# Openings of five stages: two weight splits on GpSimd, the mean in another place, one more split ahead

## The reference, cut to what matters

```python
h = h + 0.5 * rmsnorm_2(swiglu(rmsnorm_2(h, g[0]), w_ffn_in, w_ffn_out), g[1])
hn = rmsnorm_2(h, g[2])
mix = gla_mixer(hn, ...)            # or swa_mixer
h = h + rmsnorm_2(mix, g[3])
# rmsnorm_2: x * rsqrt(mean(x * x) + EPS) * g
```

## Time and profile before

| | us |
|---|---|
| median of 3 runs | 1802.15 (1801.6 to 1804.75) |
| profiled execution, its own time | 1803.02 |
| its span in the trace | 1801.2 |
| PE busy | 1742.8 (97%) |
| DVE busy | 1236.5 (69%) |
| ACT busy | 915.5 (51%) |
| POOL busy | 138.5 (8%) |
| mean granted clock of PE | 0.986 |

### The profile page before, as it was taken

One profiled execution on the slowest core, in us unless ns is written; L12 is line 12 of the kernel. 1 busy time (PEld: TensorE's weight loads), 2 busy tenths in 40 slices (PEclk: granted clock), 3 DMA queues, 4 the chain that ended last, 5 costly groups with the idle time before them and its releaser, 6 DMA issues.

```text
span 1801.2 us, 32903 instructions
## 1 busy us (share of the span) xinstructions
PE 1742.8 (97%) x13432; PEld 1646.8 (91%) x13432; DVE 1236.5 (69%) x2050; ACT 915.5 (51%) x1612; POOL 138.5 (8%) x179
## 2 busy tenths in 40 slices
PE   7999999998899999999999999999999998999998
PEld 6999999888589998999989889999899996699998
DVE  7977786765877666766466468665676657777664
ACT  7656455433764455544445445444554545555442
POOL 2001320200010001000010021000200011020001
PEclk9999999998999999999999999999999998999999
DMA  5215656541035556555544234555455562145553
GB/s 174 83 35 188 233 179 199 187 137 63 1 119 187 187 189 206 170 174 175 191 137 152 73 116 162 173 172 193 144 176 185 190 200 93 48 152 188 187 192 125
DMA packets 76469, 276.34 MB, mean 153 GB/s; under 512 B 8672, under 2 KB 9824, under 8 KB 76192
## 3 DMA queue, kind: packets, MB, share of 16 engines
q1 hardware_dynamic: 75168, 270.57, 45.4%
q0 software_dynamic: 288, 2.30, 0.4%
q10 hardware_dynamic: 864, 1.38, 0.2%
HBM read 273.16 MB, written 1.05 MB: 152 GB/s over the span
## 4 chain that ended last, share of the span: by engine, by line
PE 82%; DVE 13%; ACT 2%; issue 2%; DMA 2%; ACTq 0%; DVEq 0%
PE acc L1921 43%; PE mix L1921 18%; PE acc L1917 5%; PE acc L1918 3%; DVE scr L413 3%; DVE wl L2202 2%; DVE xl L2214 2%; DMA arrived<-in_w 1%; DVE x L2240 1%; PE acc L1941 1%; DVE y L2234 1%; PE mix L2007 1%; PE mix L807 1%; PE acc L1963 1%; ACT wh L2060 1%
## 5 line engine op out<-in xcount | busy, mean ns | idle before, releaser
L2202 DVE TENSOR_TENSOR wl<-arrived,wh 128x1024 fp32r<-128x1024 f32 x514 | 636.4, 1238 | 378.2 <-ACT wh L2060 363.5
L2060 ACT ACTIVATE wh<-arrived 128x1024 fp32r<-128x1024 f32 x514 | 540.7, 1057 | 569.7 <-DMA arrived<-in_w 569.1
L1921 PE MATMUL acc<-xh,wh 128*128 128x256 f32 (+1 forms) x1504 | 431.6, 287 | 0.4 <-DVE wl L2202 0.2
L1921 PE MATMUL acc<-xh,wl 128*128 128x256 f32 (+1 forms) x1504 | 428.5, 285 | 0.0
L1921 PE MATMUL acc<-xl,wh 128*128 128x256 f32 (+1 forms) x1504 | 428.2, 285 | 0.0
L1921 PE MATMUL acc<-hx,wh 128*128 128x256 f32 (+1 forms) x1664 | 302.9, 283 | 0.0
L1921 PEld LDWEIGHTS acc<-xh,wh 128*128 128x128 f32 x1504 | 286.0, 190 | 5.2 <-issue 3.6
L1921 PEld LDWEIGHTS acc<-xh,wl 128*128 128x128 f32 x1504 | 286.0, 190 | 0.0
L1921 PEld LDWEIGHTS acc<-xl,wh 128*128 128x128 f32 x1504 | 284.9, 189 | 0.2
L1921 PE MATMUL mix<-xh,wh 128*128 128x256 f32 (+1 forms) x960 | 274.1, 286 | 0.9 <-DVE wl L2202 0.9
L1921 PE MATMUL mix<-xh,wl 128*128 128x256 f32 (+1 forms) x960 | 272.8, 284 | 0.0
(11 more groups left out here) (450 smaller groups left out, 2248.0 us busy)
## 6 DMA issues: line engine op xcount, KB each, us to landing
arrived<-in_w SPq DMA_DIRECT2D x514, 512.0 KB, 3.3
scr<-in_cmp_w POOLq DMA_DIRECT2D x1, 2048.0 KB, 9.6
x<-in_x ACTq DMA_DIRECT2D x4, 272.0 KB, 7.4
out<-x SPq DMA_DIRECT2D x8, 128.0 KB, 1.7
par<-in_par ACTq DMA_DIRECT2D x1, 235.0 KB, 7.8
scr<-in_positions POOLq DMA_DIRECT2D x1, 128.0 KB, 7.0
scr<-in_cmp_w POOLq DMA_DIRECT2D x1, 32.0 KB, 10.9
scr<-in_w_gate POOLq DMA_DIRECT2D x1, 32.0 KB, 2.2
```

What stands on the lines that cost most here:

```text
L1921: ins = nc.tensor.matmul(bank(name, t)[:, 0:L - c], w_part[:, h.slot, w], v_part[:, k, c:], start=(k == 0 and w_part is wh and v_part is h ...
L2060: nc.scalar.activation(wh[:, h.slot, :], raw(h.slot), ACT.Copy).then_inc(w_hi, 1)
L2202: nc.vector.tensor_tensor(wl[:, h.slot, :], raw(h.slot), wh[:, h.slot, :].bitcast(F32), ALU.subtract).then_inc(w_lo, 1)
```

## The change

In every opening (u = 5 to 9), b is the last half of the stage before.

- The low parts of halves b+4 and b+5 are made by POOL (`split_low`), behind its sum for the norm that ends the stage. DVE makes neither any longer; it waits for both behind its `xl` (`wait_ge(w_lo, b + AHEAD + 1)`). ACT makes the high parts of both one behind the other, ahead of the first `xh`.
- For u = 6, 7 and 9 (`SUMMED`), ACT and DVE also split half b+6 in the opening, behind the squares and behind `xl`; the call further on in the stage that did so before is skipped (`early`).
- For u = 6, 7 and 9 the next norm's mean keeps its two products and POOL's sum, and moves behind all low products of the opening; at u = 7 behind tile 0 of ffn4_a.
- For u = 5 and 8 POOL makes no sum for the next norm; `mean_of_squares` makes the mean on PE from the 8 squares, ahead of the low products.
- `SUMS` renumbers the counts of `sum_ok`.

```diff
@@ -90,6 +90,9 @@
+OPENS = {5: "gla_lr", 6: "ffn3_a", 7: "kv", 8: "swa_q", 9: "ffn5_a"}
+
+
 def last(name):
     return BASE[name] + SIZE[name]
 
@@ -246,6 +249,19 @@
         def spread(c):
 
             return stat[:, SPREAD + c:SPREAD + L]
+
+        SUMMED = (6, 7, 9)
+        _order = [norm_of(u) for u in range(5)]
+        for _u in range(5, upto + 1):
+            _order += [norm_of(_u, True)] + ([norm_of(_u)] if _u in SUMMED else [])
+        SUMS = {v: n + 1 for n, v in enumerate(_order)}
+
+        def last_half(u):
+            return BASE[OPENS[u]] - 1
+
+        def early(b):
+
+            return b in [last_half(u) + 1 for u in SUMMED]
 
         def held_back(u, m, part):
 
@@ -1888,12 +1904,21 @@
                         step(ins)
                 ins.then_inc(sum_ok, 1)
 
+            def split_low(h):
+
+                pool.wait_ge(w_hi, h.n + 1)
+                pool.wait_ge(w_lo, h.n)
+                pool.tensor_tensor(wl[:, h.slot, :], raw(h.slot), wh[:, h.slot, :].bitcast(F32), ALU.subtract).then_inc(w_lo, 1)
+
             for u in range(0, upto + 1):
                 if u in mixers.get("pool", {}):
                     mixers["pool"][u](pool, step)
                 if u >= 5:
                     norm_sum(norm_of(u, True), c0(u))
-                if u < upto:
+                    if u < upto:
+                        split_low(Half(last_half(u) + AHEAD - 1))
+                        split_low(Half(last_half(u) + AHEAD))
+                if u < 5 or u in SUMMED:
                     norm_sum(norm_of(u), c0(u))
                 if u in mixers.get("pool_late", {}):
                     mixers["pool_late"][u](pool, step)
@@ -1953,9 +1978,9 @@
                     bank_free(pe, name, t)
                     for k in range(KD):
                         high(name, t, k)
-                for n, (name, t) in enumerate(group):
-                    if norm is not None and n == (1 if norm == 5 else 2):
-                        mean(norm_of(norm), c0(norm))
+                if norm is not None and norm not in SUMMED:
+                    mean_of_squares(norm_of(norm), c0(norm))
+                for name, t in group:
                     slot = (BASE[name] + t) % RING
                     for k in range(KD):
                         if (name, t) == group[0]:
@@ -1964,8 +1989,16 @@
                                                start=False, stop=(k == KD - 1))
                     ins.then_inc(used, 1)
 
+            def mean_of_squares(v, c):
+
+                pe.wait_ge(root_ok, v)
+                for k in range(KD):
+                    pe.wait_ge(sq_new, 8 * v + k + 1)
+                    ins = nc.tensor.matmul(stat[:, 0:L - c], ones[:], sq[:, k, c:], start=(k == 0), stop=(k == KD - 1))
+                ins.then_inc(mean_ok, 1)
+
             def mean(v, c):
-                pe.wait_ge(sum_ok, v + 1)
+                pe.wait_ge(sum_ok, SUMS[v])
                 if v:
                     pe.wait_ge(root_ok, v)
                 nc.tensor.matmul(stat[:, 0:L - c], ones[:], sumsq[:, c:], start=True, stop=False)
@@ -2024,12 +2057,16 @@
                         opening_by_tile(group[1:], cg(u), (x_lo, 0))
                 else:
                     opening(group, xh, xl, cg(u), (x_hi, 8 * u), (x_lo, 8 * u), norm=u)
+                    if u in SUMMED:
+                        mean(norm_of(u), c0(u))
 
             for u in range(0, upto):
                 f = FFN_AFTER.get(u)
                 if u == 7:
                     kv_pe(pe, gemm, opening, mean)
-                    gemm("ffn4_a", xh, xl, cg(u), (x_lo, 8 * u), last=4)
+                    gemm("ffn4_a", xh, xl, cg(u), (x_lo, 8 * u), last=1)
+                    mean(norm_of(u), c0(u))
+                    gemm("ffn4_a", xh, xl, cg(u), None, first=1, last=4)
                     for i in range(4):
                         kv_turned(pe, i)
                         gemm("ffn4_a", xh, xl, cg(u), None, first=4 + 8 * i, last=12 + 8 * i)
@@ -2061,7 +2098,7 @@
 
             def ahead(b):
 
-                if b + AHEAD < HALVES:
+                if b + AHEAD < HALVES and not early(b):
                     split(Half(b + AHEAD))
 
             def high_x(u, k):
@@ -2148,6 +2185,7 @@
                     if u >= 5:
                         rooted_by_token(norm_of(u, True), c0(u))
                         ahead(b - 1)
+                        ahead(b)
                     if u == 7 and u < upto:
                         for k in range(KD):
                             stream_new(act, u, k)
@@ -2159,7 +2197,10 @@
                                 squares(x, norm_of(u), k // 2, c0(u))
                         for k in range(KD // 2, KD):
                             squares(x, norm_of(u), k, c0(u))
-                    ahead(b)
+                        if u in SUMMED:
+                            split(Half(b + AHEAD + 1))
+                    if u < 5:
+                        ahead(b)
 
             gains = COL["conv_w"]
             act.dma_start(par[:, 0:gains], a["par"][:, 0:gains]).then_inc(in_gain, 16)
@@ -2242,17 +2283,15 @@
                 for n in range(len(GROUPS)):
                     scaled(n)
                     add(n)
-                ahead(b - 1)
                 if u == 7 and u < upto:
                     for k in range(KD):
                         kv_low(dve, k)
-                else:
-                    for k in range(KD):
-                        low_x(u, k)
-                ahead(b)
-                if u == 7 and u < upto:
-                    for k in range(KD):
-                        low_x(u, k)
+                for k in range(KD):
+                    low_x(u, k)
+                if u < upto:
+                    dve.wait_ge(w_lo, b + AHEAD + 1)
+                if u in SUMMED:
+                    split(Half(b + AHEAD + 1))
 
             def ffn(f, u):
                 name = f"ffn{f}_a"
```

## The result

The changed kernel took 1819.78 us (median of 4 executions, 1814.29 to 1823.06) against 1802.19 before (the three executions of the table above and one more): 17.6 us more, a ratio of 1.0092 with an interval of 1.0063 to 1.012. The forecast was slower, 1809.9 us, at most 1817. The direction was right, the size was not.

A forecast was written before the change was run, and what follows sets the result against it. PE, busy 97% of the span, was taken as the bound, but the openings' chain hardly runs through it. Openings 5 to 9 gave 2.4 + 2.1 - 0.7 + 1.8 + 2.1 = +7.7 us on 1802.15: 1809.9 us, range 1796 to 1817.

The forecast's parts named there:

- Who may run beside whom: In the openings, a DVE instruction with two SBUF inputs and a reading GpSimd one exclude each other for the whole instruction.
- The price of a split: A GpSimd weight split of 1024 columns takes 2.40 us, by a line through the 272- and 512-column rows.
- Openings 6 and 9: `x` complete 3.3 us later, the spared DVE split of 1.14 us off the path: +2.1 us each.
- Openings 5 and 8: Later `xh`, then a mean of 8 float32 products on PE: +2.4 us in 5, +1.8 us in 8.
- the end of the high products: Opening 5: PE's high products end 0.75 + 2.0 us behind the last `xh`, at 933.5; in opening 8 at 1507.8.
- Opening 7: PE's waits for POOL's sum (3.28 us) and a weight half (0.86 us) go, a new wait eats most: -0.7 us.
- The clock: A shorter idle stretch behind opening 5 against new gaps before `xh`: set at nothing, ends -1.7 and +6.8 us.
- the -1.7 set against the gaps: Behind opening 5, PE work lost to the clock's fall could come back as the idle stretch shrinks to 0.9 us.
- Rival 3: As forecast, and the clock falls in most openings as well: 1814 to 1818 us, chance 0.11.

The follow-up runs named there:

- experiment 2: The kernel before with the two GpSimd weight splits alone, no mean moved, no further half split ahead: 1816.92 us against 1802.16, ratio 1.0082.
- experiment 6: The kernel before plus four unused two-input GpSimd adds of 512 columns per opening, beside `x += y`: 1811.64 us against 1804.32, ratio 1.004.
- experiment 7: The kernel before plus nine unused GpSimd memsets of 512 columns per opening, beside `x += y`: 1807.63 us against 1804.32, ratio 1.0027.
- experiment 12: The changed kernel with opening 7's mean also made by PE from the 8 squares: 1817.79 us against 1803.05 for the kernel before, ratio 1.0084.
- experiment 5: The changed kernel plus idle PE products ahead of the first three tiles' high products in each opening: 1814.76 us against 1804.32 for the kernel before, ratio 1.0062.
- experiment 3: The kernel before with the mean's moves alone, both splits on DVE, no further half split ahead: 1806.33 us against 1802.16, ratio 1.002.

## Why the forecast was right in direction and wrong in size

**Who may run beside whom: right.** `x += y` was held back to GpSimd's end and 0.3 us more, twice in each opening. Experiments 2, 6 and 7 show that it is the reading GpSimd work that does it. The Trainium skill, "SBUF — State Buffer", section "Who interferes with whom", has the same rule for the reading side, and these rows agree with it.

**The price of a split: right.** 2.365 us against 2.40 from the line through two rows.

**Openings 6 and 9: right**, +2.1 and +2.5 against +2.1. PE's high products there end ahead of `xl` in turn with POOL, so even a fall of the clock costs little: opening 9 had one and is 0.4 us over.

**Openings 5 and 8: the path was right, two terms were not.** The two stages are 1.6 and 1.5 us over the forecast. One term is the clock: its fall made the mean 0.8 us later in opening 5 (experiment 12's trace against this one) and 1.2 in opening 8 (experiment 5's). The other is the end of the high products. The prediction had it at the last `xh` and 0.75 + 2.0 us more, as if PE had caught up by then. It had not: the `xh` come in pairs every 1.39 us, 0.43 us apart within a pair, and the 12 products of a pair take 1.5. In the openings without a fall the mean starts 0.75 us (5) and 0.65 us (8) later than forecast; in opening 8 some 0.35 of it is made up further on.

**Opening 7: wrong by 2.7 us.** The prediction had POOL's sum in turn with `xl` from the start, so that tile 1 starts at 1303.3 behind the mean. The timelines of POOL and DVE after:

```profile
1298.98 3.88 POOL L1899 TENSOR_TENSOR sumsq<-sq 128x272 f32<-128x272 f32 x1 [7.83 <-ACT sq L2119]
1302.93 5.03 POOL L1902 TENSOR_TENSOR sumsq<-sumsq,sq 128x272 f32<-128x272 f32 x5
```

```profile
1295.54 3.39 DVE L1604 SCALAR_TENSOR_TENSOR hx<-x,par,hx 128x272 fp32r<-128x272 f32 x8
1298.84 3.39 DVE L2255 SCALAR_TENSOR_TENSOR xl<-x,par,xh 128x272 fp32r<-128x272 f32 x8
```

DVE came first and had eight `xl` ready one behind the other (0.42 us each), and POOL's first add, 0.77 us when free, stood outside for all of them: it ended at 1302.86, 0.6 us behind the last `xl`. The sum ended at 1307.97 and the mean at 1309.2. This opening stands 3.5 us later than before (1283.3 against 1279.9), so by the times of before the mean ended at 1305.7, not 1303.3, and tile 2, which began at 1314.10, at 1310.6 instead of 1307.9. The fall of the clock in 1291 to 1296 lay under this wait and cost nothing (stage 7 is as long in experiment 5).

**The clock: the step that failed.** "I set the two against each other at nothing" was the wrong choice. The gaps of 1.1 and 1.5 us ahead of `xh` were followed by a fall in four of five openings in the changed kernel and in experiment 2, and in three of five in experiment 12; in the eleven traces of the other kernels, experiment 5 with the gaps filled among them, no high products of any opening had one. The fall behind opening 5 stayed although the idle stretch ahead of it shrank to 0.87 us, so the -1.7 set against the gaps did not come. Gaps are not the whole rule: experiment 7 had two falls among low products, where PE had waited no more than 0.5 us at a time, and what spared opening 6 is not known.

In the profiled execution the clock cost 0.8 + 1.2 + 0.4 = 2.4 us in openings 5, 8 and 9. In sum: 7.7 as forecast, 2.7 in opening 7, 1.1 for the end of the high products (0.8 and 0.3) and 6.1 of the clock are 17.6 us. The last figure is the remainder.

Two other numbers bear it out, both roughly: the 17.6 - 10.4 = 7.2 of experiment 5, and the mean granted clock, 0.981 over the four executions against 0.9845 over 29 of the kernel before, by which the clock withheld 34.5 instead of 27.9 us, 6.6 more (an estimate, span x (1 - clock); PE is not busy through all of it).

The 3.7 us of it that the profile does not show lie outside the profiled execution, which was the fastest: the other three had mean granted clocks of 0.983, 0.980 and 0.977 and took 1817.96, 1821.61 and 1823.06 us, against 0.984 and 1814.29. They left no trace, so where in them it lies stays open. Rival 3, the forecast with falls in most openings, 1814 to 1818 us, came nearest.

## What to carry to other kernels

Before a two-input instruction is handed to GpSimd, look at what DVE has to issue beside it: a DVE instruction with two SBUF inputs waited to the end of a reading GpSimd one that was ahead of it, so a critical one of 0.44 us became 2.1. The same work in instructions a quarter as long cost nothing that can be told, and on DVE, with the first half split in a place where DVE waits anyway, the kernel was 8 us faster than before, in part by fewer falls of the clock. A new PE wait of a microsecond in front of a dense run is to be priced with a fall of the clock and not with zero: 1.5 us where PE was busy throughout (24 products in 4.62 us instead of 3.11), 0.8 and 1.2 where it would have waited in between, nothing where another engine ended later. And a moved mean drags its queue along: what stands behind it on the same engine has to be made ahead of it (experiment 3).

## What the runs showed of the hardware

- The exclusion of DVE and GpSimd is not fair. An unbroken run of eight DVE instructions of 0.42 us kept one GpSimd add out for 3.1 us (opening 7), while in opening 6 the two went in turn at 0.93 us an `xl`. There each `xl` had to wait for its own `xh` or followed POOL; what decides between the two patterns was not settled.
- GpSimd that only writes (memset) does not hold back a DVE instruction with two SBUF inputs, nor is it held back: 0.44 us under it, as when alone, and 0.524 to 0.531 us for each of 45 memsets. The Trainium skill, "SBUF — State Buffer", section "Who interferes with whom", says so, and the run agrees.
- A GpSimd instruction of 256 columns took 1.07 us on average in turn with DVE (8.60 us for eight) and held an `x += y` back by 0.07 us; one of 1024 took 2.37 and held it back by 1.5 to 1.7.
- Falls of the granted clock vary in number and place between executions. The part ahead of opening 5 is nearly the same work in all kernels; over the 14 traces the clock withheld between 10.2 and 13.7 us there (11.9 in the kernel before, 10.2 in the changed one), and with all else that varies it took from 911.68 to 918.48 us.
